# Weighing the first layer's expert rows by products with diagonal weight matrices, in place of scaling, adding and transposing

## What is computed

```python
D_MODEL, SEQ, CTX_LEN, TOP_K = 1024, 1024, 256, 2
...
def expert_dispatch(h, e_idx, w, w1, w3, w2):
    ...
    ys = lax.map(run_block, (xs, block_e)).reshape(n_slots, D)
    return jnp.einsum("tkd,tk->td", ys[dest].reshape(T, TOP_K, D), w)
...
        y = hier_moe(tokens, ...)
        x = x + mod[5] * y[:Bn * L].reshape(Bn, L, D)
        if need_ctx:
            ctx = ctx + mod_c[5] * y[Bn * L:].reshape(ctx.shape)
...
        # next layer
        h = modulate(x, norm_mix[i], mod[0], mod[1])
```

## Time and profile before

| what | us |
|---|---|
| three runs, median (lowest to highest) | 2305.67 (2303.86 to 2306.35) |
| the profiled execution: its time | 2303.92 |
| the profiled execution: its span | 2302.1 |
| busy: TensorE, TensorE weight loads, DVE, ACT, POOL | 2146.8, 1198.7, 989.8, 765.1, 232.7 |

### The profile page before, as it was taken

The page is one execution under the profiler, slowest core; times in us unless marked ns, Lnnn a source line. Parts: engine busy times, 40 slices in busy tenths (PEclk is TensorE's granted clock), DMA queues, the critical chain, the costliest instruction groups (busy, mean ns, idle before and its releaser), DMA issues. The chain is left out here.

```text
span 2302.1 us, 33766 instructions
## 1 busy us (share of the span) xinstructions
PE 2146.8 (93%) x14210; PEld 1198.7 (52%) x14210; DVE 989.8 (43%) x1511; ACT 765.1 (33%) x1163; POOL 232.7 (10%) x157
## 2 busy tenths in 40 slices
PE   7999998989998999999999989998987999999897
PEld 5788885545684555555555445443764333333222
DVE  6333226655326544445445363766535222222221
ACT  5411105554214444444434354655324101000000
POOL 0010000000000000000000202452000111112110
PEclk9999999999999999999999999999998999999999
DMA  9201108007707999999999721003438999999995
GB/s 356 65 28 37 37 17 357 1 18 276 265 3 306 390 409 427 427 426 425 427 427 426 272 93 37 28 19 133 140 127 319 411 408 391 407 398 412 415 412 237
DMA packets 142620, 587.43 MB, mean 255 GB/s; under 512 B 25764, under 2 KB 62336, under 8 KB 117248
## 3 DMA queue, kind: packets, MB, share of 16 engines
q1 hardware_dynamic: 116960, 516.48, 55.8%
q0 software_dynamic: 13328, 40.91, 5.5%
q10 hardware_dynamic: 12176, 27.81, 3.2%
HBM read 529.06 MB, written 62.39 MB: 257 GB/s over the span
## 5 line engine op out<-in xcount | busy, mean ns | idle before, releaser
L2288 PE MATMUL ph<-w,x_t 128*32 128x512 f32 x4288 | 479.4, 599 | 16.8 <-DMA w<-in_exp_w 16.8
L2288 PEld LDWEIGHTS ph<-w,x_t 128*32 128x32 f32 x4288 | 135.8, 111 | 306.5 <-issue 301.4
L2325 PE MATMUL py<-w,g_t 128*32 128x512 f32 x2144 | 248.4, 604 | 9.9 <-DMA w<-in_exp_w 7.2
L2543 DVE TENSOR_TENSOR hidden<-hidden,ph 64x512 f32<-64x512 f32 x68 | 73.8, 1085 | 377.3 <-ACT hidden L2458 376.4
L2458 ACT ACTIVATE hidden<-ph 64x512 f32<-64x512 f32 x68 | 40.2, 591 | 556.4 <-PE ph L2288 556.4
L2534 DVE TENSOR_TENSOR w_low<-w,w_high 128x1024 fp32r<-128x1024 f32 x156 | 180.5, 1219 | 11.8 <-ACT w_high L2444 11.7
L2842 PE MATMUL z<-hT,w_cd 128*128 128x512 f32 (+1 forms) x448 | 183.8, 567 | 0.0
L830 PE MATMUL z<-h_high,w_hi 128*128 128x512 f32 (+1 forms) x432 | 160.0, 370 | 3.9 <-DVE h_low L925 3.5
L2444 ACT ACTIVATE w_high<-w 128x1024 fp32r<-128x1024 f32 x156 | 152.1, 1048 | 18.4 <-PE ph L2298 16.8
L832 PE MATMUL z<-h_high,w_lo 128*128 128x512 f32 (+1 forms) x432 | 155.5, 360 | 0.0
L831 PE MATMUL z<-h_low,w_hi 128*128 128x512 f32 (+1 forms) x432 | 155.4, 360 | 0.0
(11 more groups left out here) (394 smaller groups left out, 3078.6 us busy)
## 6 DMA issues: line engine op xcount, KB each, us to landing
w<-in_exp_w SPq DMA_DIRECT2D x187, 2048.0 KB, 25.6
ada_raw<-in_ada_w SPq DMA_DIRECT2D x13, 2048.0 KB, 8.1
y_slots<-zero SPq DMA_DIRECT2D x29, 512.0 KB, 14.6
late_pieces<-in_ada_w SPq DMA_DIRECT2D x5, 2048.0 KB, 14.9
h_tokens<-h_rows ACTq DMA_DIRECT2D x18, 512.0 KB, 2.6
w_ab<-in_w_in_ab SPq DMA_DIRECT2D x14, 512.0 KB, 3.9
y_slots<-y_rows ACTq DMA_DIRECT2D x26, 256.0 KB, 10.7
y_slots<-y_rows ACTq DMA_DIRECT2D x52, 128.0 KB, 8.9
```

The costliest lines, as they stand in the source:

```text
L2288: ins = pe.matmul(ph[row:row + UNIT, :], xt[:, k, at:at + UNIT], up_of(place[u + n])[:, half, k, :], start=(k == 0), stop=(k == KT - 1))
L2325: ins = pe.matmul(py[bufs[i][0]][row:row + UNIT, :], gt[:, k, n * UNIT:(n + 1) * UNIT], down_of(place[u + n])[:, k, half * 512:(half + 1) ...
L2543: dve.tensor_tensor(hid[PAIR:P, :].rearrange("s (k q) -> s q k", k=FT), hid[0:PAIR, :].rearrange("s (q k) -> s q k", k=FT), ph[PAIR:P, :]. ...
```

## The change

The scaling on ACT and the scaled sum on DVE go. In their place stand twenty small operations at the start of the block: ACT writes ten 128x128 diagonal matrices of first weights into `xl`, DVE ten of second weights into `pp[1]` and `kept`, each the identity times a column of weights. The turn becomes, for each of eight slices, two ordinary float32 products that add up in PSUM: the `ya` slice against the first diagonal, then the `yb` slice against the second. It waits for both gathers itself.

```diff
+            weights_a = [xl[:, t * P:(t + 1) * P] for t in range(NT)]
+            weights_b = [pp[1][:, t * P:(t + 1) * P] if t < 8 else kept[:, 2, 512 + (t - 8) * P:512 + (t - 7) * P] for t in range(NT)]
...
                 def turn(t):
-                    pe.wait_ge(c_wb, t + 1)
+                    pe.wait_ge(c_wa, 1)
+                    pe.wait_ge(c_wb, 1)
+                    pe.wait_ge(s_ya[t % NB], 16 * (t // NB + 1))
                     if t >= 2:
                         pe.wait_ge(c_x, t - 1)
+                    pe.wait_ge(s_yb[t % NB], 16 * (t // NB + 1))
                     for k in range(KT):
-                        ins = pe.transpose(turned[t % 2][:, k * P:(k + 1) * P], yb[:, t % NB, k * P:(k + 1) * P], self.c("ident"))
+                        here = slice(k * P, (k + 1) * P)
+                        pe.matmul(turned[t % 2][:, here], ya[:, t % NB, here], weights_a[t], start=True, stop=False)
+                        ins = pe.matmul(turned[t % 2][:, here], yb[:, t % NB, here], weights_b[t], start=False, stop=True)
                     ins.then_inc(c_t, 1)
...
-                def scale(t):
-                    act.wait_ge(s_ya[t % NB], 16 * (t // NB + 1))
-                    act.activation(ya[:, t % NB, :], ya[:, t % NB, :], ACT.Copy, scale=self.wgt[:, 0, t:t + 1]).then_inc(c_wa, 1)
...
-                scale(0)
-                scale(1)
+                for t in range(NT):
+                    ins = act.activation(weights_a[t], self.c("ident"), ACT.Copy, scale=self.wgt[:, 0, t:t + 1])
+                ins.then_inc(c_wa, 1)
                 for t in range(4):
-                    scale(t + 2)
                     square(t)
...
             def _(dve):
+                for t in range(NT):
+                    ins = dve.tensor_scalar(weights_b[t], self.c("ident"), self.wgt[:, 1, t:t + 1], None, ALU.mult)
+                ins.then_inc(c_wb, 1)
                 dve.memset(gw[:], 0.0).then_inc(s_zero, 1)
...
-                def added(t):
-                    dve.wait_ge(c_wa, t + 1)
-                    dve.wait_ge(s_yb[t % NB], 16 * (t // NB + 1))
-                    dve.scalar_tensor_tensor(yb[:, t % NB, :], yb[:, t % NB, :], self.wgt[:, 1, t:t + 1], ya[:, t % NB, :],
-                                             ALU.mult, ALU.add).then_inc(c_wb, 1)
...
-                added(0)
                 for t in range(5):
-                    added(t + 1)
                     new_x(t)
                 mean(0)
-                added(6)
                 inverse(0)
```

More of the change, by code:

```diff
@@ L2945, in _ @@
                 copy_rows(3)
-                scale(6)
                 root_of_mean(0)
@@ L2951, in _ @@
                 copy_rows(4)
-                scale(7)
                 square(5)
@@ L2955, in _ @@
                 copy_rows(5)
-                scale(8)
                 square(6)
                 copy_rows(6)
-                scale(9)
                 square(7)
@@ L3036, in _ @@
                 scaled(0, range(KT // 2, KT))
-                added(7)
                 new_x(6)
-                added(8)
                 new_x(7)
-                added(9)
                 new_x(8)
```

## The result

The changed kernel takes 2330.6 us in the median of four runs (2328.19 to 2332.16); the kernel before, run beside it, 2305.99 (2303.86 to 2306.35, four runs). The ratio is 1.0108, with a 95% interval of 1.0086 to 1.0129: slower by 24.6 us. A second measurement gave 2328.56 against 2307.2, 1.0093 (1.0073 to 1.0113), or 21.4 us. The forecast was 2325.0, 19.3 us more than before.

A forecast was written before the change was run, and what follows sets the result against it. TensorE was busy 93% of the kernel; DVE set the touched tiles' pace, TensorE close behind. 27.0 - 6.8 - 0.9 = +19.3 us, 2325.0 against the median; own range 2321 to 2332, 8-in-10 range 2319 to 2334.

The forecast's parts named there:

- The delay reaches the end: From the second layer's opening onward: a microsecond lost there counts as one lost at the kernel's end.
- A pair of load and product costs 0.11: TensorE's turns: 32 instructions at 0.11 us make 3.52 against 0.82, so 27.0 us more for ten turns.
- loads and streams in turn: Rival, TensorE's turns: loads and narrow products do not overlap, a turn takes 6.91 us, sum +53.2, 2359; chance 0.08.
- a product as cheap as a transpose: Rival, the turns: 128-column products pass as cheaply as transposes, 1.73 us a turn, sum +1.4, 2307.1; chance 0.06.
- 6.8 and 0.9 us are given back up to the first spread: First chunk: longer turns fill 6.8 us of TensorE waits up to fold 3; an earlier reciprocal returns 0.9.
- the doubtful part: TensorE's clock ahead of the first spread: it stays at its upper level, giving back 1.8 of the 6.8 us.
- Behind the first spread nothing is given back: Two long TensorE waits for ACT's squares, 8.2 us, and the half rate after stay; turns 6 to 9 count in full.
- Costed at nothing: Diagonals on ACT and DVE, 2.7 us each, inside waits for first gathers; gathers keep up; extra waits taken as nothing.
- the three more waits in each turn: Ahead of each turn, on events long past: taken as nothing, bounded by 0.22 us, 2.2 us for ten turns.
- That distance kept up to the end: Behind the second spread: its 19 us lag stays unchanged up to the expert-weight request, near 1740, and is lost at the end.
- its upper part: Whole-kernel upper ends: +22.5 us at 0.12 a pair, +24.3 with first clock loss kept, +26.5 with the waits' bound.

The follow-up runs named there:

- experiment with one product per slice: The change without its `ya` product, first expert's rows left out; 2424.34 us, total not comparable because tokens go to other experts, opening 86.2 us.
- change with filled waits: The change plus eight dummy products, three behind the first spread and five behind the second; 2322.99 us against the kernel before's 2307.19, ratio 1.007.
- kernel before with filled waits: The kernel before plus dummy products in TensorE's two long waits, three behind the first spread, five behind the second; 2301.78 us against 2306.62, ratio 0.9976.
- ident experiment: The kernel before with each turn's eight transposes made ordinary float32 products with the identity, scaling and sum unchanged; 2313.47 us against 2307.2, ratio 1.0026.
- delays: The kernel before plus dummy products ahead of the fourth projection unit: 23 took 2326.75 us against 2307.2, again 2328.76; 25 took 2329.36, beside 2304.95.

## Why the prediction was right

**The delay reaches the end.** Right: 19.8 us of dummies put in came out as 19.6. Between the opening and the router the difference changes by 0.1 us in the mean. One ground given for it was misread, though: the 50.54 of the earlier trace rows is the time from the first of four requests to the end of the last, not idle time ahead of them. SyncE's rows ahead of that request, in the kernel before:

```profile
1665.42 0.43 SPq L1371 DMA_DIRECT2D w_early<-in_exp_w  x1
1717.74 0.38 SPq L1778 DMA_DIRECT2D router_w<-in_router_gw  x1
...
1720.03 0.43 SPq L1782 DMA_DIRECT2D rank_rows<-in_k_ranks  x1
```

The queue issued nothing for 51.9 us ahead of the router's weights, so the step holds by other rows than the one named.

**A pair of load and product costs 0.11.** Right: 0.112 in the change, 0.111 in the product against the identity. The lines `L2763` and `L2764` together hold 320 instructions, 32 a turn:

```profile
L2763 PE MATMUL pa<-x_conv,y_a x80: 272/275/422, 1311.1 to 1366.6; 128*128 128x128 f32 x80
...
L2763 PE MATMUL pxg<-x_conv,y_a x80: 272/275/377, 1315.6 to 1374.5; 128*128 128x128 f32 x80
```

A row's 0.275 us is one instruction from start to end; they overlap, and the distance of their starts is what counts. The Trainium skill, page TensorE: Matmul & The Clock Gate, section Terms, has the transpose four times as fast; two instructions at 0.112 against one of 0.82/8 = 0.10 make a factor of 2.2 at these 128 columns, and the measurement decides. The rivals of loads and streams in turn, and of a product as cheap as a transpose, fall with this row.

**6.8 and 0.9 us are given back up to the first spread.** Nearly right. 27.0 x 0.6 - 7.7 = 8.5 was forecast, 9.3 measured by the block's clock; 0.35 of that is that the first row landed later by this clock. From its landing to the load of fold 3 are 1340.12 - 1311.10 = 29.02 us, so 19.19 + 6 x 2.70 - 29.02 = 6.4 of the 6.8 came back; tiles 5.30 us apart where 5.25 was forecast account for most of the rest. The spread follows that load by 1.19 us, forecast 1.18. The clock, which I called the doubtful part, stayed at 1.00 in the first two profiles of the change, behind waits for `yb` of 1.7 and 2.1 us where I had 1.34. In the third it fell there, and in the second profile of the kernel before it had not. So this term of 1.8 us came out right in part by luck.

**Behind the first spread nothing is given back.** Right: the waits for squares 8.2 us in all, as before, the second spread 20.2 later where 19 was forecast.

**Costed at nothing.** The diagonals, 3.0 us on ACT and 2.1 on DVE, lie inside the wait for the first gather, and the experiment with one product per slice, which writes them all, bounds them, together with everything else that it changes, at 3.0 us. The gathers kept up: after turn 0 no turn waits for a landing. TensorE is idle for 0.1 of the 30.3 us up to the first spread, so the three more waits in each turn cost nothing there.

**"That distance kept up to the end".** Here a step fails, by a few microseconds. Up to the request for expert weights it holds, 21.1 us later where "near 1740" was forecast. But I had counted only what the change delays, and not that 240 more rows of products move everything behind them within TensorE's program. In the router that brought a break into the 128 small products at a worse place, and the router took 5.1 us more in the mean of three profiles: 1.9 up to the end of the small products, where the break stands, and 3.2 behind it, at a clock that had fallen. Ahead of the small products the granted clock of the router does not set the kernels apart: 0.83, 0.83 and 0.89 in the change, 0.86, 0.89 and 0.83 before.

The total is +24.6 and +21.4 us in the two measurements where I had +19.3: some 1.2 from the opening and the rest from the router, by less than the profiles give it. Both lie inside the range, but its upper part was made of dearer pairs, a clock loss kept and a price for the waits; that it also held a break in the router is luck.

## What to carry to other kernels

Before moving work onto an engine, compare its own work per tile with the pace of the tile: here 2.55 of 3.27 us were TensorE's already, so relief for DVE could give back 0.7 us a tile and the products asked for 2.7. A float32 product of 128 columns is paid by its two instructions, 0.22 us with its loads, against 0.10 for a transpose. Waits behind which TensorE falls to half rate can be worth filling: eight dummy products in two such waits gained about 5 us in the kernel before. And 16 more rows of products ahead can decide on microseconds far behind: in the change they moved a break out of 128 small products, and the router took 62.2 us in place of 66.5 to 70.1.

## What the runs showed that was not expected

**TensorE's program comes in pieces, and it shows.** A run of 128 small products, done in 1.5 us, breaks for 0.5 to 3.7 us at a place that shifts one for one with 16 products put ahead, and repeats after 128 products. The traces show what it waits for. The profile counts packets of instructions by queue. The line of queue 8 on the page of the kernel before, on that of the change, and over the break alone in the third profile of the change, 1789.9 to 1793.4 (packets, MB, share):

```profile
q8 instruction: 116, 1.90, 0.3%
```

```profile
q8 instruction: 118, 1.93, 0.3%
```

```profile
q8 instruction: 1, 0.02, 1.7%
```

A packet of queue 8 is 16 KB, and the change, with 240 rows of products more, has two packets more. By the traces' packet records, in each of the ten breaks of the table, in nine profiles, TensorE goes on 1.2 to 1.5 us after such a packet has ended. In the third profile of the change TensorE stops at 1789.89, the packet runs from 1791.04 to 1791.98, and TensorE goes on at 1793.37. So the break is, by these records, a wait for the next piece of program.

This also says why the change with filled waits breaks at -19 and not again at 109: the packet ahead of that product had ended 1.4 us before it, and for the kernel before with filled waits, at 99, it was 5.0 us. In the ident experiment and the delays it was 2.7 us or more at the places reckoned above. And it says why the break is long in the change: the 128 products ahead of it, nearly all small, are 1.9 us of work, where those ahead of the 115th in the kernel before are 3.8 to 4.6. What sets the start of a packet stays open; in two profiles of the change it starts 1.2 and 1.5 us after TensorE stopped, in the first 1.3 us ahead of that.

The Trainium skill, page Runtime: NRT & Kernel Launch, section Instruction fetch mechanics, has each engine's instructions refilled in blocks of 256, over a DMA queue of the engine's own; 128 loads with 128 products are 256, so the period in the table agrees. The page adds that crossing into the next block is mostly hidden. Here it is, where slower work shares the block with the small products, and it is not at the 125th, where the block went by in 1.9 us.

**The clock falls after some waits and not after others of the same length.** Behind 2.73 us ahead of turn 0 the kernel before fell to 0.91 in its first profile; in its third, behind 3.1 us, it fell too; in its second, behind 3.0 us, it stayed at 1.00:

```profile
1304.80:1326.00 21.20, 15.27 (x132) 1.00 1.05 382
```

So a term like the 1.8 us for the clock, taken from one profile, is partly that execution's own. The single runs of one kernel spread accordingly: 2297.23 us at a mean granted clock of 0.978 and 2316.21 at 0.964, both of the kernel before with filled waits. That is why a difference of 5 us needed 12 runs.
